# A decoder trunk on one core: the first FFN pair with its own order of products and norm sums by columns, and the memory's values transposed into another PSUM bank

## What is computed

```python
def rms_norm(x, g):
    xf = x.astype(jnp.float32)
    y = xf * lax.rsqrt(jnp.mean(xf * xf, axis=-1, keepdims=True) + RMS_EPS)
    return (y * g.astype(jnp.float32)).astype(x.dtype)
...
def swiglu(h, w_in, w_out):
    g, u = jnp.split(h @ w_in, 2, axis=-1)
    return (jax.nn.silu(g) * u) @ w_out
...
def cross_attn(h, mk, mv, w_q, w_o):
    bn, L, _ = h.shape
    q = (h @ w_q).reshape(bn, L, CA_HEADS, CA_HEAD_DIM)
    o, _ = attend(q, mk, mv, jnp.ones((L, mk.shape[1]), dtype=bool))
    return o.reshape(bn, L, -1) @ w_o
...
        xp = xp + cross_attn(rms_norm(xp, norm_ca[l]), mk, mv, w_ca_q[l], w_ca_o[l])
        xp = xp + swiglu(rms_norm(xp, norm_ffn[l]), w_ffn_in[l], w_ffn_out[l])
```

## Time and profile before

| | us |
|---|---|
| median of three runs | 2957.42 |
| lowest and highest | 2957.23, 2957.85 |
| profiled execution | 2957.89 |
| its span | 2956.1 |
| TensorE busy | 2862.3 (97%) |
| VectorE busy | 1620.9 (55%) |
| ScalarE busy | 796.3 (27%) |
| GpSimd busy | 1341.0 (45%) |

### The profile page before, as it was taken

The page is one execution under the profiler, slowest core; times in us unless marked ns, Lnnn a source line. Parts: engine busy times, 40 slices in busy tenths (PEclk is TensorE's granted clock), DMA queues, the critical chain, the costliest instruction groups (busy, mean ns, idle before and its releaser), DMA issues. The chain is left out here.

```text
span 2956.1 us, 58175 instructions
## 1 busy us (share of the span) xinstructions
PE 2862.3 (97%) x21217; PEld 2723.1 (92%) x21217; DVE 1620.9 (55%) x3281; ACT 796.3 (27%) x1832; POOL 1341.0 (45%) x1156
## 2 busy tenths in 40 slices
PE   8999999999899999999999999999998999999998
PEld 7888999999899999999987778988997999999997
DVE  6554642258755655655943335522478565565565
ACT  4333422132212222112323344212323211222113
POOL 3222344435656666655431111443336665666665
PEclk9999999999999999999999999999999999999999
DMA  3101133421111111111122221243311111111112
GB/s 132 36 29 36 57 121 118 153 73 44 43 43 57 43 57 50 50 43 57 61 72 79 79 72 65 90 145 121 109 44 43 50 50 43 56 43 56 45 55 72
DMA packets 52541, 198.96 MB, mean 67 GB/s; under 512 B 6960, under 2 KB 14000, under 8 KB 49080
## 3 DMA queue, kind: packets, MB, share of 16 engines
q1 hardware_dynamic: 38736, 133.25, 14.2%
q10 hardware_dynamic: 13680, 63.97, 5.9%
HBM read 184.34 MB, written 13.10 MB: 67 GB/s over the span
## 5 line engine op out<-in xcount | busy, mean ns | idle before, releaser
L577 POOL TENSOR_TENSOR w_lo<-w_raw,w_hi 128x512 fp32r<-128x512 f32 x492 | 688.4, 1409 | 245.1 <-ACT w_hi L1381 220.1
L573 POOL TENSOR_SCALAR w_hi<-w_raw 128x512 fp32r<-128x512 f32 x324 | 210.0, 661 | 1135.9 <-PE linear L724 871.9
L724 PE MATMUL linear<-h_hi,w_hi 128*128 128x344 f32 x1110 | 366.3, 330 | 15.4 <-POOL w_lo L577 10.5
L724 PE MATMUL linear<-h_hi,w_lo 128*128 128x344 f32 x1110 | 356.2, 321 | 0.0
L724 PE MATMUL linear<-h_lo,w_hi 128*128 128x344 f32 x1110 | 356.2, 321 | 0.0
L724 PE MATMUL linear<-hid_hi,w_hi 128*128 128x344 f32 x1056 | 338.4, 320 | 2.8 <-POOL w_lo L577 1.7
L724 PE MATMUL linear<-hid_hi,w_lo 128*128 128x344 f32 x1056 | 338.6, 321 | 0.0
L724 PE MATMUL linear<-hid_lo,w_hi 128*128 128x344 f32 x1056 | 338.2, 320 | 0.0
L2433 DVE TENSOR_TENSOR x<-linear,x 128x344 f32<-128x344 f32 x480 | 246.9, 515 | 144.2 <-PE linear L724 141.8
L1045 PE MATMUL ps_scores<-c,w_hi 128*128 128x258 f32 x1584 | 306.9, 286 | 17.6 <-issue 9.7
L1045 PEld LDWEIGHTS ps_scores<-c,w_hi 128*128 128x128 f32 x1584 | 248.2, 191 | 19.4 <-issue 10.5
(11 more groups left out here) (385 smaller groups left out, 6536.3 us busy)
## 6 DMA issues: line engine op xcount, KB each, us to landing
w_raw<-in_w SPq DMA_DIRECT2D x246, 512.0 KB, 3.5
kv_slotc<-in_mem_cache_k ACTq DMA_DIRECT2D x8, 2048.0 KB, 8.3
kv_slotc<-in_mem_cache_v ACTq DMA_DIRECT2D x8, 2048.0 KB, 9.8
kv_slot<-in_dil_k ACTq DMA_DIRECT2D x4, 1536.0 KB, 6.6
kv_slot<-in_dil_v ACTq DMA_DIRECT2D x4, 1536.0 KB, 6.2
out_y<-answer SPq DMA_DIRECT2D x6, 688.0 KB, 3.5
x<-in_x ACTq DMA_DIRECT2D x2, 1376.0 KB, 10.1
out_dil_v_out<-v ACTq DMA_DIRECT2D x4, 516.0 KB, 3.6
```

Source lines behind the costliest of these rows:

```text
L573: pool.tensor_scalar(out, src, 1.0, 0.0, ALU.mult, ALU.add).then_inc(sem["hi_split"], 1)
L577: return pool.tensor_tensor(out, src, hi.bitcast(F32), ALU.subtract).then_inc(sem[event], 1)
L724: mm = pe.matmul(out, w[:, slot, cols], a, start=(k == 0 and j == 0), stop=(k == n - 1 and j == 2))
```

## The change

**The first pair of each layer** gets a program of its own (`first_pair`). The order of products is B11, B21, T2, T1, T3, B22, T4, and the first four are interleaved by halves of the inner length (kp 0 and 1, then kp 2 and 3), so that parts that exist early run first. The products use seven banks: T3 opens none and runs on in the bank of T2, B22 in that of B11, and T4 in that of T2 and T3. VectorE reads T1's bank twice, once for each sum that B22 would else have carried on. Of the seven high parts of the weights GpSimd makes the first two, and ScalarE the other five (`first_cast`). `LO_ORDER` and the order of values, joins and low parts in `combine` change with it: both B21 values are made before the fifth tile's addition, two square sums come later, the last two tiles' squares lie in SBUF (`sq_last`), and one combination less is made (`MADE` 36).

**The norm by columns.** ScalarE squares `rs_ca` once (`rs_ca2`), VectorE multiplies the summed squares by it (two halves of 516), with eps in the sums' start value. TensorE sums over channels with a single column of ones, so that the sums stand in nine columns, tokens on partitions (`column_roots`). ScalarE takes roots of 6 and 3 columns, VectorE reciprocals of them, ScalarE makes nine diagonal pieces from them, TensorE spreads these over all partitions (`spread_roots`), and ScalarE copies the three tiles into `rs`. The table loads for Sqrt and Silu are brought forward by an activation of one element each.

**In all pairs** the bank waits of the opening products are {7: -3, 0: -2, 3: -1, 4: 0, 5: -5, 6: -4}, and GpSimd waits at a turn's first pair for the low parts up to (3, B22).

**The memory's values** are transposed into `ps_t[:, 512:1024]`. T of block 0 no longer waits for `v_ready`; V of block 0 does.

The core of the diff:

```diff
+FIRST_ORDER = (0, 2, 1, 4, 3, 6, 5)
+FIRST_BANKS = {0: (7, 0), 2: (1, 2), 1: (3, 4), 4: (5, 6), 3: (3, 4), 6: (7, 0), 5: (3, 4)}
+FIRST_STEPS = [(0, 0), (2, 0), (0, 1), (2, 1), (1, 0), (4, 0), (1, 1), (4, 1), (3, 0), (3, 1), (6, 0), (6, 1), (5, 0), (5, 1)]
+FIRST_READS = (0, 1, 2, 3, 4, 6, 5)
+FIRST_CASTS = (1, 4, 3, 5, 6)
...
-                                pe.wait_ge(sem["freed_dve"], at("freed_dve", ph, i, {7: -9, 0: -2, 3: -3, 4: -2, 5: -1, 6: 0}[bank]))
+                                pe.wait_ge(sem["freed_dve"], at("freed_dve", ph, i, {7: -3, 0: -2, 3: -1, 4: 0, 5: -5, 6: -4}[bank]))
...
+                def column_roots():
+
+                    pe.wait_ge(sem["root_scaled"], at("root_scaled", f"norm_ffn{l}", 0, 2))
+                    pe.wait_ge(sem["freed_dve"], at("freed_dve", f"ffnpre{l}", 0, 2 * FIRST_READS.index(0) + 1))
+                    for t, j, o, m, n in TILE_COLUMNS:
+                        mm = pe.matmul(ffn_columns[0:m, n:n + 1], rs[:, o:o + m], ones[:, 0:1], start=True, stop=True)
+                    mm.then_inc(sem["summed"], 1)
...
+            def first_roots(l, ahead):
+
+                ph = f"norm_ffn{l}"
+                act.wait_ge(sem["col_inverted"], at("col_inverted", ph, 0, 1))
+                for t, j, o, m, n in TILE_COLUMNS:
+                    mm = copy(diagonal_ffn[0:m, t, P * j:P * j + m], ident[0:m, 0:m], scale=col_inv[0:m, n:n + 1])
+                    if j == 2:
+                        mm.then_inc(sem["diagonal"], 1)
+                act.activation(inv[:, 1:2], eps[:, 0:1], ACT.Silu)
+                for t, (a, b) in enumerate(TILES):
+                    if t == 2:
+                        ahead()
+                    act.wait_ge(sem["spread_out"], at("spread_out", ph, 0, t + 1))
+                    copy(rs[:, a:b], ffn_spread_banks[t][:, 0:TILE]).then_inc(sem["rsqrted"], 1)
...
-                            mm = pe.transpose(ps_t[:, MEM * m + P * c:MEM * m + P * c + P], vc[h][:, c, P * m:P * m + P], ident[:])
+                            to = 512 + MEM * m + P * c
+                            mm = pe.transpose(ps_t[:, to:to + P], vc[h][:, c, P * m:P * m + P], ident[:])
```

More of the change, by code:

```diff
@@ L133, in tile_plan @@
     if name.startswith("ffnpre"):
-        return pair
+        return [(b, "dve") for product in FIRST_ORDER for b in FIRST_BANKS[product]]
     if name.startswith("ffnend"):
@@ L862, in step @@
                     else:
+                        if kind == "mem" and job == 0:
+                            pe.wait_ge(sem["v_ready"], at("v_ready", phase, turn, part + 1))
                         pe.wait_ge(sem["turned_in"], at("turned_in", phase, turn, t + 1))
@@ L1600, in cross @@
                 high(2, "B11")
+                high(2, "B21")
+                made(28)
                 high(3, "B11")
+                high(3, "B21")
                 square(3, 4)
+                first_cast(l, 1)
+                first_cast(l, 4)
                 square(3, 5)
-                made(30)
+                act.activation(rs_ca2[:], rs_ca[:], ACT.Square).then_inc(sem["rs_squared"], 1)
+                made(33)
                 high(3, "T2")
-                made(32)
-                high(2, "B21")
@@ L1622, in ffn, with gates @@
             def ffn(l):
                 quarters = [(0, slice(0, HALF)), (1, slice(HALF, TOK)), (1, slice(0, HALF)), (0, slice(HALF, TOK))]
-                def gates(ph, i, p, first, ahead):
-                    for n, (c, half) in enumerate(quarters):
+                def gates(ph, i, p, first, ahead, order=quarters):
+                    for n, (c, half) in enumerate(order):
                         if n in ahead:
@@ L1644, in hid_high, with cast @@
                     copy(hid_hi[:, c, half], gate[:, c, half]).then_inc(sem["hid_hi"], 1)
-                a11, a12, a21, a22 = (w_raw[:, s, 512 * k:512 * k + 512] for s in range(2) for k in range(2))
-                block_of = (a11, w_sum[:, 1, :], a12, a21, w_sum[:, 0, :], a22, w_sum[:, 1, :])
                 sums_for = (None, 2, None, 3, 1, None, 4)
-                def cast(b, ph, i, m, raw, plain=None):
+                def cast(b, ph, i, m, raw, plain=None, later=0):
                     if b == 0:
@@ L2307, in combine @@
                                   ).then_inc(sem["t_made"], 1)
[L2308 to L2315 removed]
+                square(3, 2)
+                square(3, 3)
+                made(33)
+                join(3, "T4", "T4", ALU.subtract, "T2")
                 count[0] += 1
@@ L2331, in combine @@
                 value(2, "B22", "B22")
+                low(2, "T3")
+                first_read(l, 0)
+                low(3, "T3")
+                square(3, 4)
+                square(3, 5)
+                dve.wait_ge(sem["added"], at("added", source, 3, 6))
+                dve.wait_ge(sem["rs_squared"], at("rs_squared", ph, 0, 1))
+                for half in (FIRST, SECOND):
+                    dve.tensor_tensor(rs[:, half], rs[:, half], rs_ca2[:, half], ALU.mult).then_inc(sem["root_scaled"], 1)
```

303 lines of the change are left out of this document (203 added, 100 removed).

## The result

The changed kernel takes 2939.66 us (median; 2938.86 to 2943.41) against 2957.32 us, a ratio of 0.9945 with a 95% interval of 0.9933 to 0.9957: 17.7 us less. That is 4.3 us above the forecast of 2935.4 and inside the range of 2930 to 2947. But the sum did not come out as it was made.

| where | forecast | found |
|---|---|---|
| the eight cross-attention heads | 6.0 | 6.5, eight gaps of 0.78 gone (6.6 with all else outside the FFN) |
| the first FFN pair and the first turn of the FFN loop behind it, both layers | 16.0 | 3.65 + 3.05 = 6.7 |
| the other FFN turns, nine in each layer | 0 | 3.5 + 2.3 = 5.7 |

What follows compares the result with a forecast made beforehand. VectorE's queue was taken to set the pace in the first FFN pairs. From the median of 2957.42 us, 16.0 for two layers and 6.0 for the eight heads came off, giving 2935.4, range 2930 to 2947 (8 in 10).

Steps and rivals of the forecast that it cites:

- VectorE's sum: First FFN pair: VectorE's removed, added and moved work, GpSimd's relief and new waits sum to -8.0 us a layer.
- The new waits: First FFN pair: VectorE waits 1.0 us a layer (0 to 3.0) for the roots' 7.4 us chain through several engines.
- Does TensorE follow?: First FFN pair: TensorE is busy 32.85 of 46.22 us and 38.2 would be left, so there is room for 8.
- GpSimd's relief: First FFN pair: five high parts moved from GpSimd to ScalarE save VectorE 2.5 us a layer, bounds 0 and 3.1.
- The gap before the sums: First FFN pair: TensorE waits 2 to 4 us ahead of the column sums, and the 5.35 us gap goes.
- The other bank: Eight cross-attention heads: TensorE no longer waits for ScalarE's copy of the values, 0.70 to 0.78 us each, 6.0 in all.
- A: First FFN pairs: the chain of hands eats most of the gain, 3.5 us a layer left, 2944.4 us; chance 0.18.
- 37 to 39 us: Sign that the forecast is right: time from the first product to the third of the next pair.
- B: First FFN pairs: GpSimd's relief in full and no waits, 9.6 us gained a layer, 2932.0 us; chance 0.13.
- C: First FFN pairs: the order of products doesn't help, only the other bank's gain is left, 2951.4 us; chance 0.04.
- D: All 22 pairs: a new wait at the second product makes it slower, 2964.0 us at 1.3 a turn; chance 0.03.
- E: First FFN pairs: the table load on the roots' path also drains the engine, 1.3 x 2 us, 2938.0; chance 0.05.

Runs made afterwards that it cites:

- e2: The changed kernel with the memory values' transposes, and the wait for them, put back as they were: 2947.90 us, ratio 0.9969.
- e11: The changed kernel with four already met waits on GpSimd ahead of the second pair's first low part in the FFN turns: 2939.95 us, ratio 0.9943.
- e3: The changed kernel with 24 matmuls that nobody reads added in TensorE's gap ahead of the column sums: 2937.97 us, ratio 0.9935.
- e5: The changed kernel with its nine column sums computed twice over: 2950.43 us, ratio 0.9974.
- e10: The changed kernel with T3, T2's read and B22's cast moved ahead of the column sums or their waits, and four met GpSimd waits in FFN turns: 2936.07 us.
- e6: The changed kernel with all seven high parts of the first pair made by GpSimd again, none by ScalarE: 2942.72 us, ratio 0.9951.
- e7: The kernel before with only the FFN turns' bank waits set as late as in the changed kernel, or later: 2959.71 us, ratio 1.0007.

## Why the prediction was right, and where it was not

**VectorE's sum** held as a total: 9.0 us a layer without waits was counted, 9.1 and 8.5 were measured (9.7 and 8.8 by e2 and e11). Its relief term was too large (below), so other terms must have been too small; they were not taken apart.

**The new waits** failed: 1.0 us, with 3.0 as the bound, against 5.1 and 5.5 (idle 5.7 and 6.1, less 0.6 that were there before). Two steps led to it. First, "nine columns at 0.76 for six" read six records as six matmuls; they are three, two records each, so nine cost 2.3 us, not 1.1 (1.97 in e3 at the full clock). Second, the chain was set beside VectorE's work as if it began at once and at the full clock. In fact the sums stand behind a gap, run at 0.50 of the clock (3.60 us) and have T3's product behind them in the same queue, so VectorE's reads of T3, which were to cover the chain, had nothing to read. The question "Does TensorE follow?" was answered by busy time over the whole stretch, 32.85 of 38.2 us. But TensorE's idle time lies ahead of the sums, where it can't be used; behind them it is busy for 18.21 of 18.21 us. e3 prices the fillers, and so the clock, at 2.7 and 1.8 us a layer, e5 shows that the sums pass on in full, and e10 that the order of T3 and the sums, with the cast and the clock that it keeps up, is worth 2.8 and 3.0.

**GpSimd's relief** of 2.5 us a layer is 1.1 to 2.2 in VectorE's busy time and 0.3 and 0.7 at the end (e6). It was inside its bounds, but a relief of an engine that is about to wait is mostly swallowed.

**The gap before the sums** was forecast at 2 to 4 us and is 3.65. The reason given for the 5.35 us gap's going, "since T3's banks are T2's no longer", was false: T3 still runs in T2's banks (3, 4); what went is that the next product had to wait for a read that VectorE made late. The squares kept in SBUF cost nothing: 0.50 and 0.52 us in the trace (730.13 and 730.81), with no 1.10 on top. GpSimd was idle beside them, waiting for the cast, as argued:

```profile
737.66 1.64 POOL L593 TENSOR_TENSOR w_lo<-w_sum,w_hi 128x512 fp32r<-128x512 f32 x1 [10.55 <-ACT w_hi L1481]
```

**The other bank** was right in size and mechanism (6.0 forecast, 6.5 found).

**Rivals.** A was the mechanism that happened: each layer gains 3.5 us (4.0 and 3.0), for the reasons it named, a gap that lowers the clock and a chain of hands. It gives 2944.4; with the turns' 5.7 us off that is 2938.7, what was measured within a microsecond. So it is luck that the time came near the forecast: a gain of 5.7 us that no sum held stood in for most of the 9.3 us that the first pairs fell short. Without it the time would be about 2945.4, still inside the range, but rival A's. The sign "37 to 39 us" in the stretch was missed (42.2 and 42.4), though short of the 43 set for A. B is out (6.7, not 19.2). C is out, since the first pairs did gain. D is out: no bank gap in any turn, after or e7. E is out: the load starts 0.02 us behind the last diagonal piece (737.39 + 2.62 = 740.01, start 740.03), and the activation behind it 0.02 us behind its end (740.03 + 1.28 = 741.31, start 741.33).

**The turns** were put at nothing. Why the kernel after has no long turn, and e3 to e6, which differ from it only in the first pair, have two to six, stays open, with one execution counted of each; the runs show only that the order of two starts decides, not what moves them by 50 ns.

## What to carry over

When a chain of small steps goes through several engines, write down for each step what stands ahead of it in its engine's queue and what stands behind it: work behind it is no cover for it. Ahead of a wait put the work that doesn't need it (here T3 and one cast: 2.8 us a layer), and let TensorE have something to do in what gap remains. Ask for room on an engine piece by piece: idle time ahead of a wait is no room behind it. In a loop whose turns have two lengths, find the instruction at which they part before judging a change: here that was worth nearly a third of the change.

## What the runs showed of the hardware

Two starts 50 ns apart, in one turn only 7, decide who of VectorE (two inputs in SBUF) and GpSimd is held, and the turn is 0.65 us longer or not; four met waits on GpSimd, 0.2 to 0.4 us of delay, left no long turn in any of the four kernels that had them. A float32 matmul of one column shows as two records and costs 0.22 us at the granted clock of 1.00 (1.97 for nine) and 0.40 at 0.50 (3.60 for nine). After 3.65 us of standing still TensorE ran at the 0.50 level for the whole of the sums and for part of T3 behind them, and how long it stayed there differed by up to 1.0 us between executions with the same first pair (5.67 to 6.67 us from T3 to B22). And 24 useless matmuls, 3.2 us of TensorE's time, made each prologue 1.8 to 2.7 us shorter.
